# Up-projection by seven block products (Strassen) for half of the row tiles, plain products for the rest

## The reference, cut to what matters

```python
h = rms_norm(x, g_ffn[l])
u = h @ w_up[l]                      # 256 x 2048 by 2048 x 11264
up = jnp.pad(u, ((0, 0), (CONV_WIDTH - 1, 0), (0, 0)))
conv = sum(wc[t] * up[:, t:t + s] for t in range(CONV_WIDTH)) + b_conv[l]
gate, val = jnp.split(conv, 2, axis=-1)
x = x + (jax.nn.silu(gate) * val) @ w_down[l]    # 5632 x 2048
```

## Time and profile before

| | us |
|---|---|
| Median of 3 runs (lowest, highest) | 1414.68 (1413.87, 1415.8) |
| Profiled execution: span, first to last instruction | 1413.1 |
| Profiled execution: its own time | not given beside the span |
| TensorE busy, ScalarE busy | 1405.8, 722.2 |
| VectorE busy, GpSimd busy | 890.7, 53.0 |
| DMA | 188 GB/s over the span |

### The profile page before, as it was taken

How to read it: one execution, slowest core, us unless ns; L and a number is a source line. 1 busy time by engine, 2 the same in 40 slices (tenths; PEclk the granted TensorE clock), 3 DMA queues, 4 the chain that set the end, 5 groups by cost and what they waited for, 6 DMA issues and landing times.

```text
span 1413.1 us, 19396 instructions
## 1 busy us (share of the span) xinstructions
PE 1405.8 (99%) x6947; PEld 1184.9 (84%) x6947; DVE 890.7 (63%) x1109; ACT 722.2 (51%) x884; POOL 53.0 (4%) x65
## 2 busy tenths in 40 slices
PE   8999999999999999999999999999999999999999
PEld 7888888888888888888888888888888888888887
DVE  5646455655454456555577767676767676776765
ACT  6655444464545444444555554555454645554551
POOL 0112111110000000000000000000000000000000
PEclk9999999999999999999999999999999999999999
DMA  9865555556666655756566666666666665656652
GB/s 332 257 188 162 160 160 167 170 165 189 181 188 183 189 188 187 239 182 194 176 194 182 198 185 187 190 189 189 188 185 193 179 195 176 203 170 206 178 191 93
DMA packets 138441, 265.97 MB, mean 188 GB/s; under 512 B 10528, under 2 KB 10784, under 8 KB 137888
## 3 DMA queue, kind: packets, MB, share of 16 engines
q1 hardware_dynamic: 135488, 262.36, 60.7%
q10 hardware_dynamic: 2912, 3.06, 0.7%
HBM read 263.29 MB, written 2.10 MB: 188 GB/s over the span
## 4 chain that ended last, share of the span: by engine, by line
PE 99%; DMA 0%; DVE 0%; SPq 0%; ACT 0%; issue 0%
PE acc L327 22%; PE acc L307 20%; PE acc L309 20%; PE acc L308 20%; PE acc L324 12%; PE acc L323 1%; PE acc L348 0%; PE acc L336 0%; PE acc L359 0%; PE acc L375 0%; DMA raw<-w_in 0%; PE acc L368 0%; PE acc L437 0%; PE acc L376 0%; PE acc L356 0%; PE acc L362 0%
## 5 line engine op out<-in xcount | busy, mean ns | idle before, releaser
L815 DVE TENSOR_TENSOR w_lo<-raw,w_hi 128x1024 fp32r<-128x1024 f32 x487 | 593.7, 1224 | 466.5 <-ACT w_hi L568 463.6
L568 ACT ACTIVATE w_hi<-raw 128x1024 fp32r<-128x1024 f32 x487 | 513.5, 1058 | 558.9 <-PE acc L309 372.6
L327 PE MATMUL acc<-actB,w_hi 128*128 128x512 f32 x1320 | 466.9, 398 | 0.0
L307 PE MATMUL acc<-w_hi,actA 128*128 128x512 f32 x1116 | 442.3, 396 | 2.0 <-DVE w_lo L815 2.0
L309 PE MATMUL acc<-w_hi,actA 128*128 128x512 f32 x1116 | 435.1, 390 | 0.0
L308 PE MATMUL acc<-w_lo,actA 128*128 128x512 f32 x1116 | 434.4, 389 | 0.0
L324 PE MATMUL acc<-actB,w_lo 128*128 128x256 f32 x1408 | 391.9, 281 | 0.0
L327 PEld LDWEIGHTS acc<-actB,w_hi 128*128 128x128 f32 x1320 | 248.0, 188 | 60.4
L324 PEld LDWEIGHTS acc<-actB,w_lo 128*128 128x128 f32 x1408 | 265.9, 189 | 2.0
L309 PEld LDWEIGHTS acc<-w_hi,actA 128*128 128x128 f32 x1116 | 209.5, 188 | 44.4
L307 PEld LDWEIGHTS acc<-w_hi,actA 128*128 128x128 f32 x1116 | 209.7, 188 | 43.7 <-issue 2.4
(11 more groups left out here) (141 smaller groups left out, 591.6 us busy)
## 6 DMA issues: line engine op xcount, KB each, us to landing
raw<-w_up SPq DMA_DIRECT2D x176, 512.0 KB, 4.2
raw<-w_in SPq DMA_DIRECT2D x159, 512.0 KB, 3.9
raw<-w_down SPq DMA_DIRECT2D x88, 512.0 KB, 4.5
raw<-w_out SPq DMA_DIRECT2D x32, 512.0 KB, 4.5
raw<-w_fox SPq DMA_DIRECT2D x16, 512.0 KB, 4.5
raw<-w_dil SPq DMA_DIRECT2D x16, 512.0 KB, 4.5
work<-x_t SPq DMA_DIRECT2D x8, 256.0 KB, 6.7
work<-x SPq DMA_DIRECT2D x2, 1024.0 KB, 8.9
```

The source lines that it names most:

```text
L307: nc.tensor.matmul(o, lhsT=a_h, rhs=w_hi[:, u, k, :], start=first and k == 0, stop=False)
L327: mm = nc.tensor.matmul(banks[j][:, :], lhsT=hi_w, rhs=actB[:, kt, :], start=False, stop=kt == KT - 1)
L568: nc.scalar.activation(w_hi[:, u, :, :], raw[:, u % RAW_SLOTS, :].rearrange("p (k n) -> p k n", k=KU), ACT.Copy).then_inc(hi_done, 1)
L815: nc.vector.tensor_tensor(w_lo[:, u, :, :], raw[:, u % RAW_SLOTS, :].rearrange("p (k n) -> p k n", k=KU), w_hi[:, u, :, :].bitcast(f32), A ...
```

## The change

The columns of an up-projection block are two sides, gate (0) and value (1). Of the 16 tiles along 2048, the first eight are multiplied by a form of Strassen's scheme: the activations (two row tiles) by two halves of four k tiles, the weights two halves of k by two sides, seven products instead of eight. The other eight tiles are multiplied as before in form (plain), with three matmuls for each. The seven products need four sums of weight tiles. One (T2) is made by VectorE, three by DMAs that GpSimd issues and that add a tile of HBM to one in SBUF. The sums of activations are made once, ahead of the blocks.

In all up units activations are now stationary, so results have rows on partitions, and TensorE turns them (`turn_val`, `turn_gate`: eight squares each, to banks 4 and 7) ahead of the taps, which read PSUM. The down projection of a block is spread over later blocks. Its groups all use banks 5 and 6, except in the last two blocks. Slots of `w_hi` and `w_lo` are six. `w_up` and `w_down` lie in HBM as whole units. The loops of the gate, branch, output and feed-forward parts are written out. The order of units:

```diff
+RING = 6
...
+QU = 2
+HK = KU * QU
+PLAIN = UPR - 2 * QU
+DOWN_EARLY = 5
+STEPS = ("P3", "P1", "P7", "P6", "P5", "P2", "P4")
...
+        def down(which):
+            late = UPR - DOWN_EARLY
+            if which < DOWN_EARLY:
+                return [("D", i - 2, late + which)] if i > 1 else []
+            return [("D", i - 1, which - DOWN_EARLY)] if i > 0 else []
...
+        units += product("P3") + product("P1") + down(0) + down(1) + down(2)
+        units += product("P7") + product("P6") + down(3) + down(4) + product("P5")
+        units += [("U", i, 1, j) for j in range(PLAIN)]
+        units += product("P2") + down(5) + down(6) + down(7) + product("P4")
+        units += [("U", i, 0, j) for j in range(PLAIN)]
+    units += [("D", BLOCKS - 2, u) for u in range(UPR - DOWN_EARLY, UPR)]
+    units += [("D", BLOCKS - 1, u) for u in range(UPR)]
```

`product(name)` gives two S units. SP loads tiles for S units into `raw_x` and `raw_y`, and U and D units into the four slots of `raw`, each after the split that frees the place. TensorE:

```diff
+            def product_unit(n, part, q, o, first):
+                pe.wait_ge(lo_done, n)
+                s = n % RING
                 for k in range(KU):
+                    kt = KU * q + k
+                    a_h, a_l = part[:, kt, 0:P], part[:, kt, P:2 * P]
+                    nc.tensor.matmul(o, lhsT=a_h, rhs=w_hi[:, s, k, :], start=first and kt == 0, stop=False,
+                                     skip_group_check=True)
+                    nc.tensor.matmul(o, lhsT=a_h, rhs=w_lo[:, s, k, :], start=False, stop=False,
+                                     skip_group_check=True)
+                    mm = nc.tensor.matmul(o, lhsT=a_l, rhs=w_hi[:, s, k, :], start=False, stop=kt == HK - 1,
+                                          skip_group_check=True)
                 mm.then_inc(used, 1)
...
+            def plain_unit(n, kts, o0, o1, u0_wait):
...
+                for r, o in enumerate((o0, o1)):
+                    if r == 1 and u0_wait:
+                        pe.wait_ge(u0_copied, u0_wait)
...
+            def turn_val(i):
+                pe.wait_ge(c11_done, i + 1)
+                pe.wait_ge(c21_done, i + 1)
+                pe.wait_ge(conv_done, 2 * i + 1)
+                turn_up(val, val_ready)
...
+                    elif name == "P6":
+                        pe.wait_ge(p1_copied, i + 1)
...
+            def down_pair(i, c):
+                at = 4 * (i - BLOCKS + 2) + c
+                pairs = {2: (0, 1), 3: (2, 3), 4: (5, 6), 5: (0, 1), 6: (2, 3), 7: (4, 7)}.get(at, (5, 6))
...
+            def down_unit(n, i, u):
+                c = u // 2
+                if u == 0:
+                    pe.wait_ge(a_lo, i + 1)
+                if u % 2 == 0:
...
+                    elif i or c:
+                        pe.wait_ge(d_added, 8 * i + 2 * c)
...
+            for n, unit in enumerate(FFN, FF_UNIT):
+                if unit[0] == "D":
+                    down_unit(n, unit[1], unit[2])
+                    if unit == ("D", BLOCKS - 2, UPR - DOWN_EARLY):
+                        turn_val(BLOCKS - 1)
+                    elif unit[2] == 0 and unit[1] < BLOCKS - 1:
+                        turn_gate(unit[1] + 1)
...
+                if name == "P3" and q == QU - 1 and i:
+                    turn_val(i - 1)
```

ScalarE, after `high(n + RING)` at each unit (`high` waits for `used` of the unit six before, and for the tile or its sum):

```diff
+                    elif u == 1 and i < BLOCKS - 1:
+                        newest_tap(i + 1, 0)
+                    elif u == UPR - 1 and i < BLOCKS - 2:
+                        hidden_high(i + 1)
...
+                    if side == 0 and j == 1:
+                        gate_silu(i)
+                    elif side == 1 and j == PLAIN - 1:
+                        act.wait_ge(used, n + 1)
+                        nc.scalar.activation(gate[1], bank[0][:, :], ACT.Copy, scale=xrs2[:, 1:2])\
+                            .then_inc(u1_copied, 1)
...
+                if name == "P1" and q == 0 and i:
+                    newest_tap(i - 1, 1)
```

After P1, P6 and P5 it copies bank 0 to `val[0]` (`p1_copied`), `val[1]` (`v_copied`) and `gate[0]` (`u0_copied`). VectorE, after `low(n + RING)`, which for P7 is followed by the sum T2:

```diff
+                if n >= FF_UNIT and FFN[n - FF_UNIT][2] == "P7":
+                    dve.wait_ge(lo_done, n)
+                    nc.vector.tensor_tensor(raw_y[:, q, :], raw_y[:, q, :], raw_x[:, q, :], ALU.add)\
+                        .then_inc(t2_added, 1)
...
+            for n, unit in enumerate(FFN, FF_UNIT):
+                low(n + RING)
+                if unit[0] == "D":
+                    _, i, u = unit
                     if u % 2 == 1:
+                        add_down(n, i, u // 2)
...
+                    elif u == 2 and i < BLOCKS - 1:
+                        older_tap(i + 1, 0, 1)
+                    elif u == UPR - DOWN_EARLY and i < BLOCKS - 2:
+                        older_tap(i + 1, 1, 0)
+                    elif u == UPR - DOWN_EARLY + 1 and i < BLOCKS - 2:
+                        hidden(i + 1)
...
+                    elif side == 0 and j == PLAIN - 1:
+                        dve.wait_ge(used, n + 1)
+                        dve.wait_ge(v_copied, i + 1)
+                        result(bank[2][:, :], xrs2[:, 0:1], val[0], c11_done)
+                        result(bank[3][:, :], xrs2[:, 1:2], val[1], c21_done)
...
+                elif name == "P4" and q == 0 and i:
+                    older_tap(i, 0, 0)
+                elif name == "P1" and q == QU - 1 and i:
+                    older_tap(i - 1, 1, 1)
+                elif name == "P5" and q == QU - 1 and i:
+                    hidden_low(i - 1)
```

GpSimd issues the adding DMAs; the tiles that they fill are split next:

```diff
+            def add_tile(side, i, kt_pair, to, done):
+                nc.gpsimd.dma_start(to, w_up[1 - side, i, kt_pair, :, :], accum_op=ALU.add).then_inc(done, 16)
...
+                if name == "P3":
+                    pool.wait_ge(lo_done, n)
+                    add_tile(1, i, q, raw_y[:, q, :], y_summed[q])
+                    if i == 0 and q == QU - 1:
+                        pool.wait_ge(ms_x, 2)
+                        nc.gpsimd.tensor_tensor(xrs2, xms, mhalf[:, 0:2], ALU.pow).then_inc(rs_x, 1)
+                elif name == "P7":
+                    pool.wait_ge(t2_added, QU * i + q + 1)
+                    add_tile(1, i, q, raw_x[:, q, :], x_summed[q])
+                elif name == "P6":
+                    pool.wait_ge(lo_done, n)
+                    add_tile(0, i, QU + q, raw_y[:, q, :], y_summed[q])
```

More of the change, by code:

```diff
@@ L229, in load @@
                 n = UPR * R + u
[L230 to L234, removed]
+                if n == RAW_SLOTS:
+                    sp.wait_ge(tile_split, KU)
+                elif n > RAW_SLOTS:
+                    sp.wait_ge(lo_done, n - RAW_SLOTS)
                 s = u % RAW_SLOTS
@@ L275, in _ @@
-            with sp.Fori(0, 4) as c:
+                    load(BR0 + c, u, w[:, KU * (u % 4):KU * (u % 4) + KU, NB * c:NB * c + NB])
+            for c in range(4):
                 round_of(OUT0 + c, w_out_v, NB * c)
[L277 to L282, removed]
@@ L451, in _ @@
             pe.wait_ge(qn_done, 2 * GROUPS)
-            with pe.Fori(0, 4) as c:
+            for c in range(4):
                 for m in range(2):
@@ new lines, in _ @@
+            for n, unit in enumerate(FFN, FF_UNIT):
[5 more added lines that the diff above has]
+                        turn_gate(unit[1] + 1)
+                    continue
+                if unit[0] == "U":
+                    _, i, side, j = unit
+                    plain_up(n, i, side, j)
+                    continue
+                _, i, name, q = unit
+                if i == 0 and name == "P7" and q == 0:
+                    pe.wait_ge(x2_done, 4)
+                product(n, i, name, q)
+                if i == 0 and name == "P3" and q == QU - 1:
+                    pe.wait_ge(x2_done, 4)
+                    transpose_block(lambda r, col: xr[:, r, 3 * NB + col:3 * NB + col + P], bank[6:8], x2t_ready)
+                if name == "P3" and q == QU - 1 and i:
+                    turn_val(i - 1)
+                elif name == "P4" and q == 0 and i == 0:
+                    turn_gate(0)
@@ L969, in _ @@
                             dve.wait_ge(consts_in, 16)
-            with dve.Fori(0, 4) as c:
+            for c in range(4):
                 for m in range(2):
@@ new lines, in older_tap @@
+            def older_tap(i, side, tap):
+                q = 2 * i + side
+                ct = 4 * i + 44 * side
+                if tap == 1:
+                    dve.wait_ge(tap2, q + 1)
+                else:
+                    dve.wait_ge(tap1, q + 1)
+                lag = 2 - tap
+                for j in range(CT):
+                    t = nc.vector.scalar_tensor_tensor(
+                        out=conv[:, j, lag:SEQ], in0=bank[(4, 7)[j // 2]][:, (j % 2) * SEQ:(j % 2 + 1) * SEQ - lag],
+                        scalar=smalls_sb[:, S_WC + 88 * tap + ct + j:S_WC + 88 * tap + ct + j + 1],
+                        in1=conv[:, j, lag:SEQ], op0=ALU.mult, op1=ALU.add)
+                t.then_inc(tap1 if tap else conv_done, 1)
@@ L1067, in add_down @@
+            def add_down(n, i, c):
+                row0 = i == BLOCKS - 1 and c == 3
+                if row0:
+                    dve.wait_ge(row0_done, 1)
+                else:
+                    dve.wait_ge(used, n + 1)
                 for r in range(RT):
```

(5 more changed lines are left out.)

773 lines of the change are left out of this document (448 added, 325 removed).

## The result

The changed kernel takes 1572.95 us (median of 4 runs, 1571.63 to 1574.23) against 1415.24: a ratio of 1.112, interval 1.110 to 1.113. It is slower by 158 us, as the sign of the forecast said, and 58 us beyond its size; it lies above the range of 1464 to 1565. The profiled execution spans 1572.1 us.

What follows compares the result with a forecast made beforehand. TensorE's order, busy in 99% of 1413.1 us, was taken as the bound. 29.4 us less work and 130 us of pauses summed to +100.6, forecast 1515 us, range 1464 to 1565.

Steps and rivals of the forecast that it cites:

- TensorE's work: Feed-forward part: TensorE's own matmuls and transposes take 708.1 us against 737.5, 29.4 less; removing the loops gains nothing.
- (a): Down unit D2, right behind D1 on the same banks, waits 3.8 us for adds in blocks 1 to 10: 38 us.
- (b): Down unit D4 behind D3, same banks, VectorE late: 5.5 us in blocks 2 to 10, 50 us.
- The walk: Unit-by-unit timing of one steady block across TensorE, ScalarE and VectorE: 75.6 us a block against 66.97.
- (c): The transposes turn_val wait 1.4 us for VectorE's results in ten blocks: 14 us.
- (d): First plain up unit after P5: second half waits for ScalarE's copy of bank 0, 0.6 us, 11 times: 7 us.
- (e): End of the feed-forward part: the last block's first down unit waits for its hidden tile: 7 us, 3 to 10.
- (f): Blocks 0 and 1: P6 waits for a copy behind P5's split, which awaits a DMA sum: 14 us.
- The clock: Forecast kept the full clock; a rival had it drop at 12 pauses, 34 us on top, 1549 us, chance 0.25.
- 2 (smaller pauses): VectorE not late at D3, small waits near zero: 79 us instead of 130, 1464 us; with half, 1490; chance 0.17.
- 3 (a slow adding DMA): The accumulating DMA takes, say, 16 us, 4.6 more in ten blocks: 1561 us; chance 0.06.
- 4: Faster: the units after D1 and D3 find their banks free; 1385 us, with small waits 1400; chance 0.05.

Runs made afterwards that it cites:

- the last experiment: Changed kernel with column groups separated; adds, results, copies and last block's work ahead of splits, GpSimd's power after P7's adding DMAs: 1401.9 us, ratio 0.991.
- filled: Changed kernel with TensorE doing 14 and 20 matmuls of constant tiles in the pauses ahead of D2 and D4: 1534.6 us, ratio 1.085.
- one pair: Kernel before the change, with all four column groups of the nine looped down rounds on banks 0 and 1: 1626.2 us, ratio 1.149.
- the adds first: Changed kernel with VectorE's down-projection adds ahead of the split of their place instead of behind it: 1521.0 us, ratio 1.075.
- the groups apart: Changed kernel with each column group's two down units together and other units between groups, same banks 5 and 6: 1446.5 us, ratio 1.023.

## Why the prediction was wrong in size, point by point

**TensorE's work**: right. With nearly no waits the last experiment has 1385.1 us of busy TensorE against 1405.8 - 29.4 = 1376.4, and its clock is below full in a few stretches still. Removing the loops was to gain nothing; the feed-forward part starts 1 us earlier, and no run tells why. The six slots for split weights, down from eight, cost nothing that the waits show (0.8 us for a split in the changed kernel).

**(a) and (b)**: right. 3.83 us against 3.8, and 5.2 against 5.5; in all 82 us of wait (85 from matmul to matmul) against 88. The walk's course for VectorE ahead of D4 is there in the timeline of the changed kernel:

```profile
891.68 1.23 DVE L1022 TENSOR_TENSOR w_lo<-raw_y,w_hi 128x1024 fp32r<-128x1024 f32 x1 [0.28 <-ACT w_hi L726]
892.82 1.65 DVE L1278 SCALAR_TENSOR_TENSOR work<-acc,smalls_sb,work 128x255 f32<-128x255 f32 x4
894.39 1.21 DVE L1022 TENSOR_TENSOR w_lo<-raw_y,w_hi 128x1024 fp32r<-128x1024 f32 x1
895.52 1.28 DVE L1311 TENSOR_TENSOR work<-acc,work 128x512 f32<-128x512 f32 x2
```

A split, four operations of a tap (1.65 us together), a split, the adds, done at 896.80; D3 had ended at 891.6.

**(c)**: 1.1 us each instead of 1.4. **(d)**: 0.52 instead of 0.6, 5.7 in all against 7. **(e)**: 5.8 for the hidden tile against 5.9.

**(f)**: 14 us expected; the waits that only blocks 0 and 1 have sum to 2.2 + 9.1 + 3.6 + 2.2 = 17, and one of turn_val's is 3.2 instead of 1.1: 19 us. The mechanism named gives 9.1 of them, P6's waits. Not named were P5's two waits for the copy that follows P6 (3.6) and two of 2.2 us: the transposes of x2 for its last column group, and P4's for the first block's result. That the sum came near 14 is in part luck. Power and adding DMAs on GpSimd:

```profile
679.95 1.62 POOL L1442 TENSOR_TENSOR st<-st,smalls_sb 128x2 f32<-128x2 f32 x1 [16.09 <-DVE st L1266]
681.54 1.79 POOL L1431 DMA_DIRECT2D raw_x<-w_up  x2
```

ScalarE, from the split of P5 to the copy:

```profile
687.08 1.06 ACT L726 ACTIVATE w_hi<-raw_x 128x1024 fp32r<-128x1024 f32 x1 [5.26 <-DMA raw_x<-w_up]
...
689.61 1.06 ACT L726 ACTIVATE w_hi<-raw_x 128x1024 fp32r<-128x1024 f32 x1 [0.95 <-DMA raw_x<-w_up]
690.57 0.67 ACT L991 ACTIVATE tmp<-acc,st 128x512 f32<-128x512 f32 x1
```

GpSimd issues P7's additions only after its power, so P5's tile is split at 687.08, and the copy that P6 waits for comes at 690.57.

All of TensorE's waits together: 126 us in the feed-forward part against 130. The sum of -29.4 and 130 was thus right to 4 us, and the expected signs came: 19 waits for the adds, VectorE at 61%. Only the blocks were 80.3 us apart and not 75 to 76.

**The clock**: this is the step that failed. The forecast left it at the full level and put its fall among the rivals, with a chance of 0.25 and a price of 12 x 2.8 = 34 us. It fell after each of the ten pauses of 3.8 us as well as after each of the nine of 5.2, and the extra matmul time came to 65 us, of which 58 are left for the clock. That is also the 58 us by which the forecast of 1515 fell short. The price of one pause was under the bound: 2.2 us (filled), 2.1 (one pair), 1.9 (the adds first), against 2.8. The count was wrong: 19 pauses and those of blocks 0 and 1 and the end, not 12. At 2.2 us the 19 make 42 of the 58; of the other 16, by the starts of the matmuls, blocks 0 and 1 hold some 10 and the end 2. The prediction had named a clock below 1.00 as a sign of being wrong, and it came. The profile of before had no row with a pause and what follows it, as TensorE never pauses in its feed-forward part. The rule of the Trainium skill ("TensorE: Matmul & The Clock Gate", section "What's actually happening"), that the throttled state is the default and activity lifts it, spoke for it. The traces here agree with it: half clock behind all 19 pauses, 0.50 over 3.4 us in the row above. With 19 pauses of 3.8 us and more in the forecast itself, the drop deserved the main case and not a rival's place; this is said with the result at hand.

**The rivals.** 2 (smaller pauses) fell with the waits above. 3 (a slow adding DMA) fell: they landed in 5.4 and 5.9 us, between the bounds of 4.2 and 9.5 and under the 11.4 us of room, and plain loads left the steady waits as they were. With the groups apart, and in the last arrangement, those into raw_y took 7.5 and 7.4 us, still inside the bounds. 4 named the right mechanism for a faster kernel, free banks behind D1 and D3, and it took the order of units and not the change to bring it about: with the groups apart 1446.5 us, with the other waits taken away too 1401.9, against the 1385 and 1400 given for it. The range was too narrow on top, for it held the clock's price at 12 pauses only, 34 us where 58 came.

**Not tried**: whether the seven products themselves gain, in the last arrangement, over eight plain ones. By TensorE's work they save 11 x 12 x 0.2267 = 30 us, more than the 12.6 us gained in all, but this is argued only; without them the 22 groups of transposes, 19 us, would still be there.

## What to carry to other kernels

When a PSUM bank is reused by the very next unit, the price is not the add but everything that stands ahead of the add in the order of each engine: here 3.8 us for 1.3 us of adds. Take the units of one accumulation group together, put other work between two groups, and put what TensorE waits for ahead of work that is only due later. And a pause of TensorE has to be priced with the clock behind it: here 3.8 us of waiting cost 6 on average.

## What was not expected of the hardware

A pause of 3.8 us was enough for the half clock each time (2.1 to 2.2 us more in the mean, with short and long stretches of it in turn), while one of 1.5 us in the steady blocks cost only itself, with the granted clock at 1.00 through it and after. The length of the pause alone does not settle it. In block 1, P5 waits 1.78 us both in the changed kernel and with the adds first; these are the stretches right behind that wait, in this order:

```profile
753.45:757.50 4.05, 4.02 (x11) 3.16 (x12) 4.05 (x5) 1.38 (x2) 0.00 (x0) 0.58 0.42 135
```

```profile
752.65:756.70 4.05, 4.00 (x17) 3.30 (x18) 4.05 (x5) 2.25 (x3) 0.00 (x0) 1.00 0.32 103
```

The clock reads 0.58 in the one and 1.00 in the other. No run here tells what makes the difference. Filling a pause with matmuls that nobody reads kept the clock up and made a kernel with more work 38 us faster. A DMA that adds 512 KB to a tile in SBUF landed in 5.4 to 5.9 us in the changed kernel against 4.1 for a plain load, less than the doubling for which the forecast's upper bound allowed; in the two fastest arrangements (200 and 206 GB/s over the span against 183) those into raw_y took up to 7.5.
